# The blockwise inverse of a delta rule: products, copies and updates on 64 of 128 columns

## The reference, cut to what matters

```python
L = jnp.where(strict, jnp.einsum("bhnid,bhnjd->bhnij", k_beta, k) * decay, 0.0)
rhs = jnp.concatenate([v_beta, k_beta * jnp.exp(g)[..., None]], axis=-1)
sol = lax.linalg.triangular_solve(L, rhs, left_side=True, lower=True, unit_diagonal=True)
u, w = sol[..., :dv], sol[..., dv:]
```

## Time and profile before

| | |
|---|---|
| median of the runs | 1721.3 us (1718.0 to 1726.28) |
| the profiled execution | 1735.6 us, of it the span of the trace 1733.4 us |
| PE busy in the span | 97% (VectorE 71%, GpSimd 52%, ScalarE 41%) |
| the inverse in the trace | from about 235 to 304 us |
| mean granted TensorE clock | 0.993 of full speed |

### The profile page before, as it was taken

One profiled execution on the slowest core, in us unless ns is written; L12 is line 12 of the kernel. 1 busy time (PEld: TensorE's weight loads), 2 busy tenths in 40 slices (PEclk: granted clock), 3 DMA queues, 4 the chain that ended last, 5 costly groups with the idle time before them and its releaser, 6 DMA issues.

```text
span 1733.4 us, 25780 instructions
## 1 busy us (share of the span) xinstructions
PE 1688.3 (97%) x8004; PEld 1401.3 (81%) x8004; DVE 1224.0 (71%) x3012; ACT 703.0 (41%) x1049; POOL 897.8 (52%) x710
## 2 busy tenths in 40 slices
PE   7999999989999999999999999999999999999998
PEld 6777798878888888878788788888888888888886
DVE  7878677446897887768778322212888888888886
ACT  5444465553334444434344344323433333333333
POOL 0232202223320577657667776764676776777730
PEclk9999899999999999999999999999999999999999
DMA  9832195123236444435444344448999999999994
GB/s 354 312 141 74 49 398 222 71 101 121 81 119 238 146 146 146 146 117 168 135 146 146 109 146 135 146 138 297 326 367 365 361 372 375 344 392 350 377 354 152
DMA packets 149363, 376.21 MB, mean 217 GB/s; under 512 B 32048, under 2 KB 64944, under 8 KB 146096
## 3 DMA queue, kind: packets, MB, share of 16 engines
q1 hardware_dynamic: 114480, 308.04, 50.0%
q0 software_dynamic: 34816, 67.41, 10.9%
HBM read 312.25 MB, written 63.11 MB: 217 GB/s over the span
## 4 chain that ended last, share of the span: by engine, by line
PE 89%; DVE 5%; ACT 2%; issue 2%; DMA 1%; DVEq 1%; SPq 0%; ACTq 0%
PE bank L1127 16%; PE bank L1128 16%; PE bank L1129 16%; PE bank L1562 10%; PE bank L1566 10%; PE bank L1564 10%; PE bank L1348 1%; PE bank L1335 1%; PE bank L1522 1%; DMA g_in<-gate_scratch 1%; DVE modr L1634 1%; PE bank L1227 1%; DVE small L1766 1%; PE bank L1218 0%; DVE qkvT L1704 0%
## 5 line engine op out<-in xcount | busy, mean ns | idle before, releaser
L672 POOL DMA_INDIRECT gate_scratch<-merged,idx_cell x384 | 427.9, 1114 | 254.1 <-ACT aout L1043 135.9
L1127 PE MATMUL bank<-act_hi,whi 128*128 128x512 f32 x1312 | 516.0, 393 | 4.4 <-issue 2.8
L1129 PE MATMUL bank<-act_hi,wlo 128*128 128x512 f32 x1312 | 512.3, 390 | 4.0 <-issue 4.0
L1128 PE MATMUL bank<-act_lo,whi 128*128 128x512 f32 x1312 | 512.7, 391 | 1.7 <-issue 1.5
L2037 DVE TENSOR_TENSOR wlo<-raw,whi 128x1024 fp32r<-128x1024 f32 x252 | 307.9, 1222 | 252.8 <-ACT whi L1037 202.5
L1562 PE MATMUL bank<-whi,chi 128*128 128x512 f32 x768 | 298.8, 389 | 0.5 <-DVE clo L2186 0.5
L1564 PE MATMUL bank<-wlo,chi 128*128 128x512 f32 x768 | 298.8, 389 | 0.0
L1566 PE MATMUL bank<-whi,clo 128*128 128x512 f32 x768 | 298.8, 389 | 0.0
L1127 PEld LDWEIGHTS bank<-act_hi,whi 128*128 128x128 f32 x1312 | 247.5, 189 | 59.3 <-issue 6.6
L1129 PEld LDWEIGHTS bank<-act_hi,wlo 128*128 128x128 f32 x1312 | 247.3, 189 | 55.7 <-issue 4.0
L1128 PEld LDWEIGHTS bank<-act_lo,whi 128*128 128x128 f32 x1312 | 247.3, 189 | 53.4 <-issue 3.7
(11 more groups left out here) (364 smaller groups left out, 1836.9 us busy)
## 6 DMA issues: line engine op xcount, KB each, us to landing
raw<-in_expert_tiles SPq DMA_DIRECT2D x256, 512.0 KB
act_scratch<-aout SPq DMA_DIRECT2D x128, 256.0 KB
gate_scratch<-zeros SPq DMA_DIRECT2D x24, 1024.0 KB, 21.9
a_in<-act_scratch SPq DMA_DIRECT2D x128, 192.0 KB
g_in<-gate_scratch SPq DMA_DIRECT2D x128, 192.0 KB
modr<-in_mod_tiles SPq DMA_DIRECT2D x28, 512.0 KB
raw<-in_in_tiles SPq DMA_DIRECT2D x28, 512.0 KB
raw<-in_query_tiles SPq DMA_DIRECT2D x16, 512.0 KB
```

Of the source, the lines that this page charges most:

```text
L672: g.indirect_dma_start(out=gate_cells, out_offset=bass.IndirectOffsetOnAxis(ap=idx_cell[:, b, k:k + 1], axis=0), in_=merged[:, b, k:k + 1] ...
L1127: mm(out_bank[:], whi[:, slot, w], act_hi[:, k, :], start=(k == 0), stop=False)
L1128: mm(out_bank[:], whi[:, slot, w], act_lo[:, k, :], start=False, stop=False)
L1129: last = mm(out_bank[:], wlo[:, slot, w], act_hi[:, k, :], start=False, stop=(k == KD - 1))
```

## The change

Three things are new in each of the 20 steps. `level_p` streams only the first block of each pair from `Tm` (runs of c = 2, 4, 8, 16 or 32 adjacent columns out of every 2c) and writes the 64 resulting columns of a head side by side in PSUM, so that four heads take 256 columns. ScalarE copies these 256 columns, `level_t` multiplies them, and `updated` subtracts the 256 results from the same runs of `Tm`. The weights of all matmuls stay 128x128, the transposes stay whole, and so do `masked` and the copies to `TT`. No instruction is added, removed or moved.

```diff
+        def half_of(h):
+            return slice(h * CJ, (h + 1) * CJ)
+
+        def first_runs(ap, n):
+            return ap.rearrange("p (g z c) -> p g z c", z=2, c=2 << n // NB)[:, :, 0, :]
+
+        def by_run(ap, n):
+            return ap.rearrange("p (g c) -> p g c", c=2 << n // NB)
...
-                    sc.copy(PM[:, t, :], bank[t % 2][:]).then_inc(s_pc, 1)
+                    sc.copy(PM[:, t, 0:H * CJ], bank[t % 2][:, 0:H * CJ]).then_inc(s_pc, 1)
...
-                    last = mm(bank[t % 2][:, hs(h)], LM[:, t, hs(h)], Tm[:, t, hs(h)], start=True, stop=True)
+                    last = mm(by_run(bank[t % 2][:, half_of(h)], n), LM[:, t, hs(h)],
+                              first_runs(Tm[:, t, hs(h)], n), start=True, stop=True)
...
-                    last = mm(bank[2 + t % 2][:, hs(h)], TT[:, t, hs(h)], PM[:, t, hs(h)],
+                    last = mm(bank[2 + t % 2][:, half_of(h)], TT[:, t, hs(h)], PM[:, t, half_of(h)],
                               start=True, stop=True)
...
-                tt(Tm[:, t, :], Tm[:, t, :], bank[2 + t % 2][:], ALU.subtract).then_inc(s_tm, 1)
+                new = first_runs(Tm[:, t, :], n)
+                tt(new, new, by_run(bank[2 + t % 2][:, 0:H * CJ], n), ALU.subtract).then_inc(s_tm, 1)
```

## The result

| | before | after |
|---|---|---|
| median of 22 runs each | 1721.28 us (1717.59 to 1726.28) | 1725.16 us (1720.32 to 1729.88) |
| ratio | | 1.0019, 95% interval 1.001 to 1.0027 |
| span of the profiled execution | 1733.4 us | 1722.3 us |
| the inverse in the trace, from the start of the two `masked` ahead of the first gap to the first L1411 (L1422 after) | 235.75 to 303.64 = 67.9 us | 238.26 to 308.40 = 70.1 us |

The forecast was 1719.6 us, 1.7 us less; the time rose by 3.9 us. The two profiled spans lie the other way round than the medians: the profiled execution of before took 1735.6 us, more than any of the 22 runs. The spans are therefore not compared; the inverse is, since it can be cut out of both traces.

A forecast was written before the change was run, and what follows sets the result against it. TensorE was taken to bound the kernel, with 89% of the chain that ended last. Savings of 0.41 + 0.53 + 0.31 + 0.10 + 0.35 = 1.70 us gave 1721.3 − 1.7 = 1719.6 us, range 1712 to 1725 us.

The forecast's parts named there:

- Pace set by the weights: Halved products on TensorE: 128x128 weights set 108.4 ns a record, so a group takes 0.867 us, 0.023 less.
- Rival A: Halved products: columns set the pace, groups near 0.61 us, about 8 us less in all, 1713 us; chance 0.08.
- Copy and update: Copies to `PM` shrink 0.22 us each, hidden by waits for TensorE; updates 0.26 each, three of 20 on the path.
- The path between the gaps: Chain from 241.09 us to the join: 0.41 + 0.53 + 0.31 + 0.10 + 0.35 = 1.70 us less.
- an unchanged pace: Case where the matmuls' pace does not move at all: 1.70 − 0.41 − 0.05 − 0.35 = 0.9 us less.
- The step from `level_t(8)` to `vk_transposes(0)`: VectorE's path from 266.04 to 271.86 us: two shorter updates, 2 x 0.26 = 0.53 us less, `masked` unchanged.
- that end: `masked` beside GpSimd's scaling of q: 0.9 us better if it escaped to the usual 0.7 us.
- The step to `vk_transposes(1)`: Waits for `updated(10)` and three scalings: VectorE's side gives 0.31 us, TensorE's 0.40; the lesser counts, 0.31 less.
- The clock: Sign in the profile after: granted clock 1.00 from 240 to 304 us; 0.50 there would make the prediction wrong.
- rival B: Thin products around the gap at 269 to 272 us let TensorE's clock fall: some 28 us more, 1747 us; chance 0.05.
- the transposes at 381 us: Evidence against a clock fall: 28 transposes alone from 381.18 us brought the clock from 1.2 to 2.4 GHz before 387.

The follow-up runs named there:

- the repeated runs: Changed kernel run again with no edit, beside the kernel before: ratio 1.003 (1.0007 to 1.0054), mean clock 0.9874 against 0.9909.
- the later transposes: v and k transposes and their scalings at steps 11, 13, 15, 17 instead of 10, 12, 14, 16: 1.0018 in the kernel before, 0.9991 in the changed kernel.

## Why the prediction was wrong, point by point

- *Pace set by the weights* (0.023 us less per group): right. A step lost 0.05 us. Rival A is out: no group of a step came near 0.61 us.
- *Copy and update*: right in size (373 and 416 ns for 368 and 417) and in being hidden.
- *The path between the gaps*: without the clock 0.9 us were gained in this trace, where 1.7 was forecast. That 0.9 was also the forecast's value for an unchanged pace is luck: two terms were wrong and nearly cancelled. The step from `level_t(8)` to `vk_transposes(0)` gave 1.4 us where 0.53 was taken, because `masked` was not stretched by GpSimd; that end was named. The step to `vk_transposes(1)` was forecast at −0.31 and came out at +1.5, because a 16-column scaling now began with nearly a whole weight split of GpSimd ahead of it. I had looked for what GpSimd could stretch only up to the first wait and not behind it.
- *The clock*: the step that failed. The prediction put "the granted clock 1.00 from 240 to 304 us", gave rival B 0.05, and priced it as one fall lasting to the end (28 us) or one of some 5 us that "would cost 3 us and not be seen". The trace of the result is close to the second, 6.8 us long and 3.2 us dear. But it is the usual case and not one in twenty, and mostly it is longer: falls of 7 to 17 us in all in each of the five traces of kernels with thin streams and the waits in place, now behind the first gap, now at the waits before the v and k transposes, sometimes both; by the mean clocks of the repeated runs 12 us more at the lower level than before, which cost 5 to 6 us and turned a gain of about 1 us into a loss of 4 to 5. The mechanism had been named, with its two ingredients (a gap, thin work beside it). I dismissed it because the transposes at 381 us had raised the clock alone. They did so after 5.4 us, and that row says how a low clock ended, not what holds a high one. The row that mattered was the other one: a stretch with 2.22 us of work in 3.40 lost the clock, one with 1.38 of denser work kept it.
- *One trace*: the trace of before had no fall in the inverse, and I read this as a margin. It was the exception: the four later traces with 128 columns each have one of 3.4 us. That falls come in some executions and at changing places could be seen only from several.

What stays open: why a fall lasts longer with thin streams, and how often each kernel has one; one trace per kernel shows lengths but no rates. That the thin streams' columns and not their reading in short runs matter is argued, not shown. That the later transposes help the thin kernel through the clock and not only through VectorE is likewise supported by the clocks of twelve runs and one trace, not separated further.

## What to carry to other kernels

Halving the columns of a float32 matmul whose weights stay 128x128 bought 0.05 us in the 1.78 us of a step's two groups on TensorE; with waits of about 2 us nearby the clock was down for longer than with full streams, and that cost more than all the saving. Take such a cut where TensorE runs without waits, or remove the waits first: here the same thin streams went from a loss of 0.2 to 0.3% to none (0.9991, up to 1.0003) by moving another piece of work by one step. Judge small changes by the mean granted clock of many executions beside their times, and a small VectorE instruction by which GpSimd instruction it will start behind, not by its usual length.

## What the runs showed of the hardware

- With 128x128 float32 weights the number of columns up to 128 hardly changes the pace: 108.4 ns a record with 1 moving column, (0.84 + 0.89) / 16 = 108 ns with 64, 111 ns with 128. With 64 columns the first product of a step reads 0.84 and the second 0.89 in the chain; the ends in it are modelled, so only the sum is meant.
- At the lower clock both thin and full-width groups took twice as long: 1.60 us for a thin one (0.84 at 2.4 GHz), 1.79 us for a full one (0.89).
- Reading and writing `Tm` in runs of 2 to 32 numbers cost VectorE nothing: 416 ns in the mean of all levels, and 417 to 423 for the four updates with runs of 2, against 417 for unstrided 256 columns (on 64 partitions).
- VectorE instructions were stretched beside GpSimd's: 512 columns of `masked` from 0.69 to 2.08 us, the 16-column scaling to between 0.33 and 2.17 us. The latter ended 0.03 to 0.04 us behind the GpSimd instruction that was running when it began, in all 14 traces.
- A fall of the clock behind a wait of TensorE of 1.8 to 2.8 us lasted 3.4 us in four traces with 128-column streams; with 64 columns single falls lasted 6.8 to 13.7 us.
